# The front of the recurrence and its receptance projection in one stage

## The chip, the cores and the metric

The kernel runs on 1 core of one Trainium2 chip. The metric is the device time of one execution in microseconds; a median over a few executions is compared.

## The reference, cut to what matters

The program computes a first transformer block, then a second model of two layers on 256 latent and 256 context tokens (D = 1024). Each layer ends in a mixture of 32 experts. The second layer's mixer is a bidirectional recurrence; what the change touches is the beginning of `rwkv_prepare`:

```python
h = rmsnorm(x, norm1_g) * (1 + sc1) + sh1          # for latents and for context
xx = h_shift - h                                   # neighbour in the grid, or in the sequence
xr, xw, xk, xv, xa = [h + xx * mu[j] for j in range(5)]
r = xr @ wr                                        # 1024 x 1024, the receptance
k = xk @ wk
v = xv @ wv
lw = tanh(xw @ w1) @ w2                            # per direction; la likewise from xa
```

All is in float32.

## The kernel before, in words

Activations lie with the channels on the partitions: `h`, `xx` and the mixed inputs are `[128, 8, 512]`, eight chunks of 128 channels by 512 tokens. Work is written as a sequence of blocks (stages); each engine runs its own list in a block, and a block ends in a barrier of all engines. `Kernel.clear` (line 216) frees the semaphores of the past stages and adds a second barrier (line 219).

Weights come through a ring of six slots of 1 MB (`Stream`, lines 66 to 128), all loaded from SP's queue in one fixed order of tiles. `feed` starts tile n + 6 when tile n has been used; `hold` stops the stream before a given tile and `resume` (line 101) starts the six held tiles at once. The order here is `rw_wr_2` (four tiles of 256 output columns, slots 0 to 3), `w1` (one tile, two DMAs), `rw_wk_2` (four), `rw_wv_2` (four), `a1`, `g1`, `g2`, `wo`.

The stages around the change, in order of time:

- `experts_stage` for layer 0 (line 2375). It ends in the combination: SP fetches the experts' rows (line 2416), ACT and DVE weigh and add them (2572, 2441), PE turns them (2544), DVE adds them to `k.x` (2454). Its last entry on SP is the resume of the weight stream, which starts `rw_wr_2`'s four tiles, `w1` and the first of `rw_wk_2`. Then comes `k.clear()` (line 2729).
- `rwkv_front` (line 2755). ACT squares the eight chunks (2767), PE sums them into bank 0 with a matrix of ones (2783), DVE and ACT form the inverse root (2818 to 2823), DVE scales each chunk (2827), ACT adds the shift (2776), POOL takes the differences `xx` (2803 to 2812), and DVE blends chunk by chunk into `xm0`, the input of the receptance (2834). SP has nothing to do here.
- `linear_stage` "rw_wr_2" (line 579 on). PE forms the eight output chunks of `r` one after the other, each over all eight input chunks in one bank, four banks in turn (line 623). DVE first computes the next mixed input into `xm1` (`mix`, line 2842, passed as `first`), then copies each finished bank to `r` (2848). SP refills a weight slot each time two output chunks are done.
- `linear_stage` "w1", then "rw_wk_2", "rw_wv_2", "a1", "g1", "g2", and the scan.

One float32 product of 128x128 by 128x512 is recorded as two matmul instructions, so the receptance's 64 products are 128 instructions.

Of the kernel before, what the change touches and what calls it, by code (L numbers as in the profile page):

```python
# [19 lines left out]
ALU = mybir.AluOpType  # L20
# [4 lines left out]
P = 128  # L25
D = 1024
DC = D // P
# [2347 lines left out]
def experts_stage(k, route):  # L2375


    nc, l, TT = k.nc, route.l, route.TT
    ring = k.ring
    pair_rows = k.pair_rows[l]  # L2380
    with ExitStack() as ctx:
# [17 lines left out]
        weighed, summed, cturned, added = (k.sem(f"cb_{n}") for n in ("weighed", "summed", "turned", "added"))  # L2399
        block = ctx.enter_context(nc.Block())  # L2400
        half_cols = lambda bank, t: bank[t * RH:(t + 1) * RH, 0:256]

        @block.sync
        def _(sp):
            for n in range(ring.SLOTS, NE * ring.PIECES):
                e, j = divmod(n, ring.PIECES)
                if n == (AFTER + 3) * ring.PIECES:
                    sp.wait_ge(spent, 4 * AFTER + 4)
                    over.sync(sp)
                done, part = divmod(n - ring.SLOTS, ring.PIECES)  # L2410
                sp.wait_ge(spent, 4 * done + (1, 1, 2, 2, 3, 4)[part])
                ring.start(sp, k.a, l, e, j)
            for s in range(2):
                sp.wait_ge(put[s], 16 * (NE // 2))
            for t in range(TT):
                sp.dma_start(pairs[t], pair_rows[4 * P * t:4 * P * (t + 1), :].rearrange("(p c n) d -> p c (n d)", c=2, n=2))\
                    .then_inc(fetched[t], 16)
            if l == 0:
                k.stream.resume(sp, k.seg["wo"].first)

        @block.vector
        def _(dve):
# [329 lines left out]
    return ["rw_wr_2", "w1", "rw_wk_2", "rw_wv_2", "a1", "g1", "g2", "wo"]  # L2752


def rwkv_front(k, parts, h, xx, sq, scratch, mixed):


    nc = k.nc
    r0, mean, rr = (scratch[:, n, :] for n in range(3))
    squared, summed, meaned, rooted, vdone, scaled, ready, edged = (k.sem(f"front_{n}") for n in (  # L2760
        "squared", "summed", "meaned", "rooted", "vdone", "scaled", "ready", "edged"))
    W, q = 64, DC // 4
    with nc.Block() as block:
        @block.scalar
        def _(act):
            for c in range(DC):
                nc.scalar.activation(sq[:, c, :], k.x[:, c, :], ACT.Square).then_inc(squared, 1)
            nc.scalar.preload_act_table_set("natural_log_exp_and_others")
            act.wait_ge(meaned, 1)
            nc.scalar.activation(r0, mean, ACT.Ln).then_inc(rooted, 1)  # L2770
            act.wait_ge(rooted, 1)
            nc.scalar.activation(r0, r0, ACT.Exp, scale=-0.5).then_inc(rooted, 1)
            for c in range(DC):
                for n, (t0, t1, _, shift) in enumerate(parts):
                    act.wait_ge(scaled, 2 * c + n + 1)
                    nc.scalar.activation(h[:, c, t0:t1], h[:, c, t0:t1], ACT.Identity, bias=shift[:, c:c + 1])\
                        .then_inc(ready, 1)

        @block.tensor
        def _(pe):  # L2780
            for c in range(DC):
                pe.wait_ge(squared, c + 1)
                last = nc.tensor.matmul(k.bank[0][:, :], k.ones[:, :], sq[:, c, :], start=(c == 0), stop=(c == DC - 1))
            last.then_inc(summed, 1)

        @block.gpsimd
        def _(pool):
            for c in range(DC):
                a, b = h[:, c, 0:SEQ], xx[:, c, 0:SEQ]
                rows = lambda x: x.rearrange("p (r w) -> p r w", w=W)  # L2790
                pool.wait_ge(ready, 2 * c + 1)
                if c < q:
                    edge, inner = (rows(b)[:, :, 0:1], rows(a)[:, :, 0:1]), (
                        rows(b)[:, :, 1:W], rows(a)[:, :, 0:W - 1], rows(a)[:, :, 1:W])
                elif c < 2 * q:
                    edge, inner = (rows(b)[:, :, W - 1:W], rows(a)[:, :, W - 1:W]), (
                        rows(b)[:, :, 0:W - 1], rows(a)[:, :, 1:W], rows(a)[:, :, 0:W - 1])
                elif c < 3 * q:
                    edge, inner = (b[:, 0:W], a[:, 0:W]), (b[:, W:SEQ], a[:, 0:SEQ - W], a[:, W:SEQ])
                else:  # L2800
                    edge, inner = (b[:, SEQ - W:SEQ], a[:, SEQ - W:SEQ]), (
                        b[:, 0:SEQ - W], a[:, W:SEQ], a[:, 0:SEQ - W])
                nc.gpsimd.tensor_scalar(edge[0], edge[1], -1.0, None, ALU.mult).then_inc(edged, 1)
                nc.gpsimd.tensor_tensor(inner[0], inner[1], inner[2], ALU.subtract).then_inc(edged, 1)
                a, b, n = h[:, c, SEQ:TB], xx[:, c, SEQ:TB], TB - SEQ
                pool.wait_ge(ready, 2 * c + 2)
                e = 0 if c < DC // 2 else n - 1
                nc.gpsimd.tensor_scalar(b[:, e:e + 1], a[:, e:e + 1], -1.0, None, ALU.mult).then_inc(edged, 1)
                if c < DC // 2:
                    nc.gpsimd.tensor_tensor(b[:, 1:n], a[:, 0:n - 1], a[:, 1:n], ALU.subtract).then_inc(edged, 1)  # L2810
                else:
                    nc.gpsimd.tensor_tensor(b[:, 0:n - 1], a[:, 1:n], a[:, 0:n - 1], ALU.subtract).then_inc(edged, 1)

        @block.vector
        def _(dve):
            link = Chain(dve, vdone)
            dve.wait_ge(summed, 1)
            nc.vector.tensor_scalar(mean, k.bank[0][:, :], 1.0 / D, EPS, ALU.mult, ALU.add).then_inc(meaned, 1)
            dve.wait_ge(meaned, 1)
            dve.wait_ge(rooted, 2)  # L2820
            link(nc.vector.tensor_tensor(rr, r0, r0, ALU.mult))
            link(nc.vector.scalar_tensor_tensor(out=rr, in0=rr, scalar=-0.5, in1=mean, op0=ALU.mult, op1=ALU.mult))
            link(nc.vector.scalar_tensor_tensor(out=rr, in0=rr, scalar=1.5, in1=r0, op0=ALU.add, op1=ALU.mult))
            for c in range(DC + 2):
                if c < DC:
                    for t0, t1, gain, _ in parts:
                        nc.vector.scalar_tensor_tensor(out=h[:, c, t0:t1], in0=k.x[:, c, t0:t1],
                                                       scalar=gain[:, c:c + 1], in1=rr[:, t0:t1],
                                                       op0=ALU.mult, op1=ALU.mult).then_inc(scaled, 1)
                if c >= 2:  # L2830
                    b = c - 2
                    dve.wait_ge(ready, 2 * b + 2)
                    dve.wait_ge(edged, 4 * b + 4)
                    nc.vector.scalar_tensor_tensor(out=mixed[:, b, :], in0=xx[:, b, :], scalar=param(k, "mu", 1, b),
                                                   in1=h[:, b, :], op0=ALU.mult, op1=ALU.add)


def mix(k, xx, h, n, to, T=TB):

    def run(dve):  # L2840
        for c in range(DC):
            k.nc.vector.scalar_tensor_tensor(out=to[:, c, 0:T], in0=xx[:, c, 0:T], scalar=param(k, "mu", 1, n * DC + c),
                                             in1=h[:, c, 0:T], op0=ALU.mult, op1=ALU.add)
    return run
# [6 lines left out]
def rwkv(k, held, more):  # L2851
    nc, a, seg = k.nc, k.a, k.seg
    with ExitStack() as outer:
# [6 lines left out]
        with ExitStack() as c2:  # L2860
# [1 line left out]
            xm1 = c2.enter_context(nc.sbuf_tensor("rw_mixed1", [P, DC, TB], F32))  # L2862
            h, xx, xm0 = (c3.enter_context(nc.sbuf_tensor(f"rw_{n}", [P, DC, TB], F32)) for n in ("h", "xx", "mixed0"))
            parts = [(t0, t1, k.gain1[:, n, :], k.mod[:, n, 0:DC]) for n, (t0, t1) in enumerate([(0, SEQ), (SEQ, TB)])]
            rwkv_front(k, parts, h, xx, xm0, xm1, xm0)

            for n, name, dst in ((0, "rw_wr_2", r), (1, "w1", lw), (2, "rw_wk_2", kx), (3, "rw_wv_2", v),
                                 (4, "a1", la)):
                xm = (xm0, xm1)[n % 2]
                following = mix(k, xx, h, n + 1, (xm0, xm1)[(n + 1) % 2], TB if n < 4 else SEQ)  # L2870
                if name in ("w1", "a1"):
                    f = ACT.Tanh if name == "w1" else ACT.Copy
                    linear_stage(k, name, seg[name], whole_tiles(DC, P), lambda f, xm=xm: xm[:, f, :], TB,
                                 lambda act, m, ps, f=f, dst=dst: nc.scalar.activation(dst[:, :], ps[:, :], f), 4,
                                 on_scalar=True, first=following)
                else:
                    linear_stage(k, name, seg[name], whole_tiles(DC, 256), lambda f, xm=xm: xm[:, f, :], TB,
                                 copy_to(nc, dst), 4, first=following)
# [933 lines left out]
```

## Time and profile before

| | |
|---|---|
| median of 3 runs | 3166.9 us (3159.68 to 3167.87) |
| the profiled execution | 3166.59 us, of which the span of the trace is 3164.9 us |
| TensorE (PE) busy | 2720.3 us, 86% of the span |
| VectorE (DVE) busy | 1071.8 us, 34% |
| ScalarE (ACT) busy | 528.0 us, 17% |
| GpSimd (POOL) busy | 325.0 us, 10% |
| DMA | 638.61 MB, mean 202 GB/s |
| mean granted TensorE clock | 0.948 of 2.4 GHz |

Busy shares are averages over some forty stages with different limits. What matters for a change in two of them is a view in order of time: which engine ends last in each, and what the next stage's first instruction waits for. "Idle before, releaser" in brackets gives how long an engine stood still before an instruction and what ended that; a q behind an engine's name (PEq, DVEq) is its sequencer, so "PEq L219" stands for a barrier at line 219.

### The profile page before, as it was taken

What the parts mean: (1) busy time and instruction counts of PE and PEld (TensorE: products, weight loads), DVE (VectorE), ACT (ScalarE), POOL (GpSimd) and SP (SyncE); (2) the same over time, 40 slices, a digit from 0 to 9 for tenths busy, and PEclk for the clock granted to TensorE, in tenths of its full rate; (3) what the DMA queues carried; (4) which work ended last, traced back from release to release, by engine and by line L of the source; (5) the groups of instructions that cost most, each with busy time, mean ns of one, the idle gap of its engine ahead of it and who ended that gap; (6) DMA issues with size and microseconds to landing.
All of it is one profiled execution on the core that took longest, in us unless ns stands there. A gap on an engine that the chain in (4) does not pass through costs nothing. (4 is left out here: it accounts for less than half of the span.)

```text
span 3164.9 us, 59020 instructions
## 1 busy us (share of the span) xinstructions
PE 2720.3 (86%) x25835; PEld 1973.8 (62%) x25835; DVE 1071.8 (34%) x2214; ACT 528.0 (17%) x1149; POOL 325.0 (10%) x358
## 2 busy tenths in 40 slices
PE   8999999989999997878776599798899987977775
PEld 7886766678868775444443244588788874544443
DVE  4563337435733213101001421465556422100002
ACT  1001132300011002000000100344444312000001
POOL 1000000000000001111110200223222202111110
PEclk9999999989999997989999799799999988999997
DMA  7785432057865237999998220000000138999994
GB/s 259 241 245 159 121 123 94 29 184 248 264 202 150 70 102 296 395 401 402 401 406 330 91 80 23 20 4 4 3 4 4 57 131 319 405 407 408 406 406 180
DMA packets 297238, 638.61 MB, mean 202 GB/s; under 512 B 29252, under 2 KB 198423, under 8 KB 262436
## 3 DMA queue, kind: packets, MB, share of 16 engines
q1 hardware_dynamic: 254896, 558.44, 48.3%
q10 hardware_dynamic: 30500, 61.96, 5.4%
q0 software_dynamic: 11600, 14.59, 1.5%
q8 instruction: 199, 3.26, 0.4%
q14 instruction: 43, 0.35, 0.0%
HBM read 634.79 MB, written 21.08 MB: 207 GB/s over the span
## 5 line engine op out<-in xcount | busy, mean ns | idle before, releaser
L2509 PE MATMUL bank<-expert_weights,ex_xt 128*64 128x256 f32 x2560 | 306.0, 386 | 79.9 <-DMA expert_weights<-in_moe_w_up_dram 61.5
L544 PE MATMUL bank<-u,weights 128*128 128x272 f32 (+1 forms) x1408 | 319.2, 390 | 12.0 <-DVEq L567 12.0
L2509 PEld LDWEIGHTS bank<-expert_weights,ex_xt 128*64 128x64 f32 x2560 | 203.2, 139 | 186.5 <-issue 121.0
L544 PEld LDWEIGHTS bank<-u,weights 128*128 128x128 f32 x1408 | 271.1, 193 | 59.9 <-DVEq L567 12.6
L1353 DVE SCALAR_TENSOR_TENSOR ada_acc<-ada_w,cond,ada_acc 128x512 f32 (+1 forms) x336 | 227.7, 747 | 1.6 <-PEq L516 1.6
L2427 DVE TENSOR_TENSOR ex_hidden<-ex_silu,bank 128x256 f32<-128x256 f32 x64 | 27.0, 421 | 572.2 <-ACT ex_silu L2558 572.2
L623 PE MATMUL bank<-rw_mixed,weights 128*128 128x512 f32 (+2 forms) x448 | 188.7, 582 | 31.9 <-DVEq L636 28.2
L2509 PE MATMUL bank<-weights,ex_xt 128*64 128x256 f32 x1280 | 163.1, 394 | 34.1 <-DMA weights<-in_moe_w_up_dram 24.1
L2530 PE MATMUL bank<-expert_weights,ex_hidden_turned 128*64 128x512 f32 x640 | 152.6, 619 | 20.7 <-DVE ex_hidden_turned L2430 20.1
L2558 ACT ACTIVATE ex_silu<-bank 128x256 f32<-128x256 f32 x64 | 24.6, 384 | 872.6 <-PE bank L2509 857.5
L623 PEld LDWEIGHTS bank<-rw_mixed,weights 128*128 128x128 f32 (+1 forms) x448 | 83.9, 189 | 137.1 <-issue 135.2
L623 PE MATMUL bank<-hidden,weights 128*128 128x272 f32 (+1 forms) x704 | 157.2, 386 | 3.8 <-DVEq L636 3.8
L2509 PEld LDWEIGHTS bank<-weights,ex_xt 128*64 128x64 f32 x1280 | 102.7, 142 | 89.4 <-issue 55.3
L623 PEld LDWEIGHTS bank<-hidden,weights 128*128 128x128 f32 x704 | 133.6, 190 | 27.4 <-DVEq L636 4.7
L3748 POOL TENSOR_TENSOR sc_n<-sc_nt,sc_masks 128x512 f32<-128x512 f32 x80 | 103.5, 1295 | 404.2 <-PE bank L3032 257.5
L2434 DVE COPY ex_y<-bank 128x512 f32<-128x512 f32 x64 | 44.3, 692 | 249.5 <-PE bank L2530 249.5
L2370 POOL DMA_INDIRECT rt_xg<-token_rows,rt_tokens x64 | 61.1, 955 | 517.7 <-PE bank L2493 398.7
L2530 PEld LDWEIGHTS bank<-expert_weights,ex_hidden_turned 128*64 128x64 f32 x640 | 43.8, 141 | 103.9 <-issue 74.0
L2462 POOL DMA_INDIRECT pair_rows<-ex_y,rt_pairs_of x64 | 65.6, 1025 | 376.4 <-DVE ex_y L2434 344.9
L3032 PE MATMUL bank<-sc_x,sc_n 64*64 64x64 f32 x2560 | 96.1, 220 | 3.1 <-POOL sc_x L3750 1.9
L3032 PEld LDWEIGHTS bank<-sc_x,sc_n 64*64 64x64 f32 x2560 | 88.7, 136 | 14.1 <-issue 14.1
L2530 PE MATMUL bank<-weights,ex_hidden_turned 128*64 128x512 f32 x352 | 83.7, 617 | 12.9 <-DVE ex_hidden_turned L2430 10.9
(612 smaller groups left out, 4312.7 us busy)
## 6 DMA issues: line engine op xcount, KB each, us to landing
expert_weights<-in_moe_w_gate_dram SPq DMA_DIRECT2D x80, 1024.0 KB
expert_weights<-in_moe_w_up_dram SPq DMA_DIRECT2D x80, 1024.0 KB
expert_weights<-in_moe_w_down_dram SPq DMA_DIRECT2D x80, 1024.0 KB
ada_w<-in_ada_w_dram ACTq DMA_DIRECT2D x24, 2048.0 KB, 9.1
weights<-in_moe_w_down_dram SPq DMA_DIRECT2D x44, 1024.0 KB
weights<-in_moe_w_gate_dram SPq DMA_DIRECT2D x40, 1024.0 KB
weights<-in_moe_w_up_dram SPq DMA_DIRECT2D x40, 1024.0 KB
weights<-in_ga_w_in_dram SPq DMA_DIRECT2D x32, 1024.0 KB, 5.8
```

The lines of the kernel that those rows point to most:

```text
L544: last = nc.tensor.matmul(k.bank[b + side * NB][:, 0:N], w[:, f, c * P:(c + 1) * P], rhs[:, f, 0:N], start=(f == 5), stop=(f == 4))
L623: last = nc.tensor.matmul(ps[:, t0:t1], view(slot), of(r), start=(starts and p == 0), stop=(ends and p == len(pieces) - 1))
L1353: last = nc.vector.scalar_tensor_tensor(out=to, in0=src, scalar=c, in1=to, op0=ALU.mult, op1=ALU.add)
L2370: pool.indirect_dma_start(route.xg[:, e % 2, :], None, route.rows, bass.IndirectOffsetOnAxis(ap=route.tokens[0:SLOTS, e:e + 1], axis=0), b ...
L2427: nc.vector.tensor_tensor(hid[:, s, :], act_out[:, s, :], k.bank[3][:, 0:256], ALU.mult)\
L2434: nc.vector.tensor_copy(y[:, s, :], k.bank[6 + s][:, :]).then_inc(kept, 1)
L2462: pool.indirect_dma_start(pair_rows, bass.IndirectOffsetOnAxis(ap=route.pairs_of[:, e:e + 1], axis=0), y[:, e % 2, :], None, bounds_check= ...
L2509: last = nc.tensor.matmul(half_cols(k.bank[2 + side], t), xt[:, s, f * SLOTS:(f + 1) * SLOTS], w[:, q * 512 + t * 256:q * 512 + t * 256 + ...
L2530: last = nc.tensor.matmul(k.bank[6 + s][n * RH:(n + 1) * RH, :], ht[:, s, o:o + SLOTS], w[:, q * D + n * 512:q * D + n * 512 + 512], start ...
L2558: nc.scalar.activation(act_out[:, s, :], k.bank[2][:, 0:256], ACT.Silu).then_inc(silued, 1)
L3032: last = nc.tensor.matmul(ps[rows, CHUNK(j)], lhsT(rows, j), rhs(rows, j), start=True, stop=True)
L3748: level_mask = lambda z, level: nc.gpsimd.tensor_tensor(chunked(q.n[:, z, :]), chunked(q.nt[:, z, :]), mask_of(q, M_LEVEL + level - 1), AL ...
```

## The change

The front and the receptance projection become one block. The resume of the weight stream moves from the end of the experts' block to SP's list in the new block, followed by the feed of `rw_wr_2`. PE takes the products in another order: for each blended chunk f it adds that chunk's part to all eight output chunks, in banks 0 to 7, and signals the outputs only in the last pass. DVE then computes the next mixed input and copies the eight banks.

```diff
@@ experts_stage, SP, after the pairs' fetches
-            if l == 0:
-                k.stream.resume(sp, k.seg["wo"].first)
@@ rwkv_front
-def rwkv_front(k, parts, h, xx, sq, scratch, mixed):
+def rwkv_front(k, parts, h, xx, sq, scratch, mixed, r, following):
...
+        @block.sync
+        def _(sp):
+            k.stream.resume(sp, k.seg["wo"].first)
+            k.stream.feed(sp, seg, made, lambda j: 2 * j + 2, 2 * seg.tiles)
...
             last.then_inc(summed, 1)
+            for f in range(DC):
+                pe.wait_ge(blended, f + 1)
+                for m in range(DC):
+                    if f == 0 and m % 2 == 0:
+                        k.stream.wait(pe, seg, 0, m // 2)
+                    w = f * 256 + m % 2 * P
+                    last = nc.tensor.matmul(k.bank[m][:, :], k.stream.slot(seg, m // 2)[:, w:w + P], mixed[:, f, :],
+                                            start=(f == 0), stop=(f == DC - 1))
+                    if f == DC - 1:
+                        last.then_inc(made, 1)
...
-                                                   in1=h[:, b, :], op0=ALU.mult, op1=ALU.add)
+                                                   in1=h[:, b, :], op0=ALU.mult, op1=ALU.add).then_inc(blended, 1)
+            following(dve)
+            for m in range(DC):
+                dve.wait_ge(made, m + 1)
+                nc.vector.tensor_copy(r[:, m, :], k.bank[m][:, :])
@@ rwkv
-            rwkv_front(k, parts, h, xx, xm0, xm1, xm0)
-
-            for n, name, dst in ((0, "rw_wr_2", r), (1, "w1", lw), (2, "rw_wk_2", kx), (3, "rw_wv_2", v),
+            rwkv_front(k, parts, h, xx, xm0, xm1, xm0, r, mix(k, xx, h, 1, xm1))
+
+            for n, name, dst in ((1, "w1", lw), (2, "rw_wk_2", kx), (3, "rw_wv_2", v),
```

## Rows read from the trace of the kernel before

**Rows 1.** Busy time by stretch: PE, PEld, DVE, ACT, POOL (us), clock, DMA share, GB/s
```profile
1750.50:1755.20 4.70, 0.00 (x0) 0.00 (x0) 0.00 (x0) 0.00 (x0) 0.00 (x0) 0.50 1.17 312
...
1764.90:1773.40 8.50, 0.01 (x1) 0.00 (x0) 6.34 (x12) 3.87 (x8) 3.03 (x6) 0.80 0.00 0
1773.40:1789.60 16.20, 0.00 (x0) 0.00 (x0) 10.92 (x17) 4.64 (x10) 15.36 (x27) 0.50 0.00 1
```

**Rows 2.** Order of time (start, us, engine, line), from the combination to the front's sum
```profile
1746.26 4.22 DVE L2454 SCALAR_TENSOR_TENSOR x<-bank,mod,x 128x128 f32<-128x128 f32 x16
...
1751.34 2.77 SPq L93 DMA_DIRECT2D weights<-in_rw_wk_dram  x1
1755.21 4.27 ACT L2767 ACTIVATE rw_mixed<-x 128x512 f32<-128x512 f32 x8 [11.69 <-PEq L219]
...
1755.89 9.01 PE L2783 MATMUL bank<-rw_mixed,ones 128*128 128x512 f32 x16 [7.53 <-ACT rw_mixed L2767]
```

**Rows 3.** Order of time, the blends: first, second and eighth of eight
```profile
1772.64 0.75 DVE L2834 SCALAR_TENSOR_TENSOR rw_mixed<-rw_xx,params,rw_h 128x512 f32<-128x512 f32 x1 [0.58 <-ACT rw_h L2776]
...
1775.47 0.84 DVE L2834 SCALAR_TENSOR_TENSOR rw_mixed<-rw_xx,params,rw_h 128x512 f32<-128x512 f32 x1 [0.94 <-POOL rw_xx L2803]
...
1788.87 0.75 DVE L2834 SCALAR_TENSOR_TENSOR rw_mixed<-rw_xx,params,rw_h 128x512 f32<-128x512 f32 x1 [1.31 <-POOL rw_xx L2812]
```

**Rows 4.** Order of time, the receptance's products, last copy, next stage's products
```profile
1790.34 56.91 PE L623 MATMUL bank<-rw_mixed,weights 128*128 128x512 f32 x128 [25.43 <-DVEq L636]
...
1847.29 0.69 DVE L2848 COPY rw_r<-bank 128x512 f32<-128x512 f32 x1 [6.18 <-PE bank L623]
...
1848.44 7.11 PE L623 MATMUL bank<-rw_mixed,weights 128*128 128x512 f32 x16 [1.20 <-ACTq L636]
```

**Rows 5.** The experts' block's end (line 2381), 1749 to 1755.5: ns, then start us
```profile
L2381 DVEq DRAIN x1: 2108/2108/2108, 1748.4 to 1748.4; - x1
L2381 SPq DRAIN x1: 123/123/123, 1754.2 to 1754.2; - x1
```

**Rows 6.** Order of time around the clear before the scan
```profile
2004.25 0.42 DVE L2891 COPY rw_gate<-bank 128x256 f32<-128x256 f32 x1 [1.88 <-PE bank L623]
2005.54 2.08 PE L3150 MATMUL bank<-rw_lw,sc_w 64*128 64x512 f32 x4 [1.33 <-PEq L219]
```

**Rows 7.** Order of time, a DVE result and the PE that waited for it
```profile
1736.05 1.28 DVE L2441 SCALAR_TENSOR_TENSOR expert_weights<-expert_weights,rt_wts 128x1024 f32<-128x1024 f32 x1 [9.47 <-ACT expert_weights L2572]
...
1737.39 1.97 PE L2544 MATMUL bank<-ident,expert_weights 128*128 128x128 f32 x8 [11.55 <-DVE expert_weights L2441]
```

**Rows 8.** Order of time, weight loads early in the receptance's products
```profile
1793.03 0.34 PEld L623 LDWEIGHTS bank<-rw_mixed,weights 128*128 128x128 f32 x1 [0.52 <-issue]
1793.87 0.19 PEld L623 LDWEIGHTS bank<-rw_mixed,weights 128*128 128x128 f32 x1 [0.50 <-issue]
1794.30 0.19 PEld L623 LDWEIGHTS bank<-rw_mixed,weights 128*128 128x128 f32 x1 [0.24 <-issue]
```

**Rows 9.** Busy time by stretch of 2 us, after the front's sum
```profile
1768.00:1770.00 2.00, 0.00 (x0) 0.00 (x0) 1.93 (x4) 0.23 (x1) 0.00 (x0) 0.99 0.00 0
1770.00:1772.00 2.00, 0.00 (x0) 0.00 (x0) 2.00 (x5) 1.77 (x5) 1.63 (x4) 0.50 0.00 0
```

**Rows 10.** SP's four issues for `wo`; DMA share in 0.75 us slices from 2470
```profile
2477.09 5.43 SPq L93 DMA_DIRECT2D weights<-in_rw_wo_dram  x4
...
DMA  0000000000179999999999999994100000000000
```

**Rows 11.** DMA issues, 1800 to 1850: count, KB, us from issue to landing
```profile
weights<-in_rw_wk_dram SPq DMA_DIRECT2D x3, 1024.0 KB, 5.2
```

**Rows 12.** Order of time, one expert: products over two banks, products in one
```profile
1711.48 3.67 PE L2509 MATMUL bank<-expert_weights,ex_xt 128*64 128x256 f32 x32 [1.44 <-DMA expert_weights<-in_moe_w_up_dram]
...
1722.18 3.65 PE L2530 MATMUL bank<-weights,ex_hidden_turned 128*64 128x512 f32 x16 [0.52 <-DVE ex_hidden_turned L2430]
```

**Rows 13.** Groups of instructions, 1789.6 to 1847.9: busy us, mean ns of one
```profile
L623 PE MATMUL bank<-rw_mixed,weights 128*128 128x512 f32 x128 | 56.9, 607 | 25.4 <-DVEq L636 25.4
```

More of the change, by code:

```diff
@@ L2752, in rwkv_segments @@
     return ["rw_wr_2", "w1", "rw_wk_2", "rw_wv_2", "a1", "g1", "g2", "wo"]
-def rwkv_front(k, parts, h, xx, sq, scratch, mixed):
-    nc = k.nc
+def rwkv_front(k, parts, h, xx, sq, scratch, mixed, r, following):
+    nc, seg = k.nc, k.seg["rw_wr_2"]
     r0, mean, rr = (scratch[:, n, :] for n in range(3))
-    squared, summed, meaned, rooted, vdone, scaled, ready, edged = (k.sem(f"front_{n}") for n in (
-        "squared", "summed", "meaned", "rooted", "vdone", "scaled", "ready", "edged"))
+    squared, summed, meaned, rooted, vdone, scaled, ready, edged, blended, made = (k.sem(f"front_{n}") for n in (
+        "squared", "summed", "meaned", "rooted", "vdone", "scaled", "ready", "edged", "blended", "made"))
     W, q = 64, DC // 4
     with nc.Block() as block:
+        @block.sync
+        def _(sp):
+            k.stream.resume(sp, k.seg["wo"].first)
+            k.stream.feed(sp, seg, made, lambda j: 2 * j + 2, 2 * seg.tiles)
         @block.scalar
```

## The prediction

> **What bounds the kernel now.** The page says that PE is busy for 86% of the span, but not where the rest is lost, so I read the stretches around the changed lines first [rows 1]. From 1750.5 to 1755.2 no engine computes and only the DMA engines move data. From 1764.9 to 1789.6 DVE, ACT and POOL work and PE stands still. From 1790.3 on PE is busy for 56.9 us without a gap [rows 4]. Each stretch has one owner, and they stand one behind another: first a barrier, then the vector side of the front, then PE.
>
> Next I read the order of time for what ends each stretch. The combination's last sum of `k.x` ends at 1746.26 + 4.22 = 1750.48, yet the front's first square starts only at 1755.21, released by the barrier of line 219; in between SP is still issuing the sixth held tile, until 1751.34 + 2.77 = 1754.11 [rows 2]. The block's own end says who is late: DVE's drain, which begins at 1748.4 and lasts 2.108 us, is over at 1750.5, and SP's begins at 1754.2 [rows 5]. So it is SP's issuing, not computing, that ends the experts' block.
>
> In the front the first blend is done at 1772.64 + 0.75 = 1773.39 and the eighth at 1789.62 [rows 3]. The receptance needs all eight only because of its order of work. Its 128 instructions run from 1790.34 to 1847.25, the last copy ends at 1847.98, and the next stage's PE starts at 1848.44 [rows 4].
>
> **Part 1, the resume leaves the experts' block.** Without SP's seven issues that block ends with DVE at 1750.48. From the last work to the first instruction behind a clear it took 1755.21 - 1754.11 = 1.10 us here [rows 2], and 2005.54 - 2004.67 = 0.87 us at the clear before the scan, where DVE was last as it will be here [rows 6]. I take 0.9: the front's first square starts at 1751.4, which is 3.8 us earlier (3.6 to 3.9 by the two rows). The fetches of the experts' rows stand ahead of the resume on the same queue, so I cost their landing at no change. From below the price of Part 1 is nothing, if POOL or ACT turned out to be as late as SP; no row shows that.
>
> The issues themselves are not gone: SP makes them at the head of the new block, where it has nothing else to do until PE's last pass. Nobody waits for SP there, only for the landings. The nearest row is `wo`: four 1 MB tiles issued into an empty queue. It took SP 5.43 us from 2477.09, and the DMA engines were busy until the slice that ends at 2491.75, 14.7 us after the first issue [rows 10]. By that the fourth receptance tile is there at 1751.4 + 14.7 = 1766.1. The first product is due at 1769.7 (below) and the seventh, the first that needs the fourth tile, later still. So the cost is nothing, with 3.5 us in hand. If the loading ran at half that pace, 29.4 us, the fourth tile would come at 1780.8; the first pass, slow as it starts, wants it 4 x 0.84 + 8 x 0.43 = 6.8 us after 1769.7, at 1776.5. That is a loss of some 4 us, and my upper bound for this part.
>
> During 1751 to 1771 the loads now lie beside squares, sum, and the first scales and differences. Before, they lay beside the combination and the squares, and eight squares took 4.27 us all the same [rows 2]. I cost this at nothing, within 0.5 us either way.
>
> **Part 2, products follow the blended chunks.** Everything in the front from the first square to the first blend keeps its order: 1773.39 - 1755.21 = 18.18 us. So blend 0 is done at 1751.4 + 18.2 = 1769.6. PE follows a DVE result within 1737.39 - 1737.33 = 0.06 us [rows 7], so products start at 1769.65 in place of 1790.34: 20.7 us earlier, of which 3.8 are Part 1's and 16.9 this part's.
>
> Does PE then run through? One warm instruction takes 1794.30 - 1793.87 = 0.43 us, a cold one 1793.87 - 1793.03 = 0.84 [rows 8]. A pass of 16 takes 6.9 us warm. The second blend is done 2.9 us behind the first and the eighth 16.2 behind it, 2.3 us each on the mean [rows 3], so PE is the slower from its first pass: blend 1 is ready 2.9 us after the start, pass 1 begins 4 x 0.84 + 12 x 0.43 = 8.5 us after it. The eight waits on `blended` find their value already there, as do the waits on the four tiles. The same number of waits (each output chunk's bank and each tile) stood in the old order, whose 128 instructions show no gap. Thus the products take 56.9 us as before: the same 128 instructions and as many weight loads, the same slow start.
>
> The slow start stays because PE still rests before it. The granted clock was 0.99 of full speed until 1770 and 0.50 from then on, 5 us after the sum's last product [rows 9]. The new gap is from 1761.1 to 1769.65, 8.5 us, so the first instructions again run at 1.2 GHz, and four of them cost 4 x 0.41 = 1.7 us extra, already inside the 56.9. Were PE still warm, the time would be 1.7 us lower; this is the lower bound of the term.
>
> Eight banks in place of four, and a new bank with each product: the nearest rows are an expert's. Its gate and up products alternate between two banks and take 3.67 / 32 = 0.115 us per 256 columns; its down products stay in one bank and take 3.65 / 16 = 0.228 per 512, the same per column [rows 12]. I cost switching at nothing. At the other end, the switch could lose the overlap between neighbours; that end is priced as a rival.
>
> The Trainium skill has two rules that speak against this loop. "TensorE: Matmul & The Clock Gate", section "HAM oscillation", advises finishing all K-tiles of an output before waiting, since a wait between K-tiles lets the clock fall in every one; its section on psum-queue depth-cycling says the same of cycling through banks with small pauses. Here the row shows the chunks coming faster than PE uses them, so the first has nothing to bite on; by either, the time would be that of the clock rival below.
>
> **Part 3, the tail of the stage.** DVE's next mix (8 instructions) starts right after blend 7, at about 1786, and ends by 1792, far before the first finished bank. Copies of 0.69 us follow outputs that now finish every 0.86 us (two instructions), so only the last copy is behind PE, as before: the stage ends 0.73 us after its last product [rows 4]. The barrier between front and receptance (0.3 us and the first wait) is gone, and is inside the 20.7.
>
> The cost of the new order is in the refills. All four slots come free in the last 5.2 us, at 1.7 us steps, where they came free 13.7 us apart. So four tiles of 1 MB are issued together; SP's last issue falls at the end of the products. [rows 10] say what four such issues take: 5.43 us from the first. These start 5.2 us before the end, so SP is free some 0.3 us after PE, before DVE's last copy; the barrier doesn't move. They are all landed 14.7 us after the first, 9.5 us into what follows. The stage `w1` uses a tile landed long ago and takes 7.1 us [rows 4]. The stage behind needs its first tile, which is the sixth held one, and its second only after another pass of 13.7 us. A single tile landed 5.2 us after its issue [rows 11]. So no wait there: cost nothing, at most 1 us if SP's last issue is held longer than in [rows 10].
>
> **Sum.** 3.8 + 16.9 = 20.7 us less. The profiled execution took 3166.6 us (span 3164.9 and 1.7 around it), so it becomes 3145.9. It lies 0.3 us under the median of the runs shown, so the forecast for a median is 3146.
>
> **Rivals.**
>
> *The barrier does not move (chance 0.07).* Some other engine or the clear itself holds the front until 1755.2. For it: idle barriers are put down to PE's sequencer in the view, which names no true culprit. Against it: SP's drain in [rows 5]. Only Part 2 is left: 3166.6 - 16.9 = 3149.7 us.
>
> *Weights late, or slower vector work beside the loads (0.06).* The bound above, 4 us: 3145.9 + 4 = 3149.9 us.
>
> *Switching banks costs (0.03).* An instruction is recorded with 0.607 us on the mean [rows 13], though they start 0.43 apart, since neighbours overlap. If nothing overlapped, 128 x (0.607 - 0.43) = 22.7 us would be added: 3145.9 + 22.7 = 3168.6 us, no gain. Against it, [rows 12].
>
> *The clock stays down, the case on the other side (0.03).* If the passes were broken by waits, so that PE stayed at 1.2 GHz, each of the 124 warm instructions would take 0.41 us more, 51 us in all: 3145.9 + 51 = 3197 us. From 50 slow instructions more on (20.7 / 0.41) the change loses. For it: in the front PE does fall to half speed when it rests. Against it: blends every 2.3 us on the mean against passes of 6.9 us. The Trainium skill's two sections named above would have this one come.
>
> **How the numbers follow.** The forecast has 0.81, the four rivals 0.07, 0.06, 0.03 and 0.03. A measurement of this kernel can't tell less than about 0.3% from no change, 9.5 us (the three runs shown lie 8.2 us apart). Forecast and the first two rivals are faster by more: 0.94. The banks' case is no change, 0.03, and the clock's slower, 0.03. For the range: above, the first two rivals reach 3150, and I add 1 us for SP's last issue; below, a warm start gives 3144, and the lowest run of before lay 7 us below the median, which puts a like one at 3139. Range 3139 to 3151.
>
> **What would show it.** ACT's first square about 0.9 us behind the last sum of the combination; SP's seven issues behind it; a product of the new line starting 18.2 us after that square, with 128 instructions in 57 us and no idle time between; clock 0.5 for its first 3.5 us and then 1.0; four refills in its last 5.2 us; `w1` starting 1.2 us after it. The prediction is wrong if the square stays at 4.7 us behind the sum, if products wait for weights, if PE idles or runs cold between passes, or if the key projection waits for its second tile.

## The result and the profile after

| | before | after |
|---|---|---|
| the pair timed first (4 runs each) | 3166.56 us (3159.68 to 3167.87) | 3134.03 us (3130.67 to 3139.49) |
| ratio | | 0.9904, 95% interval 0.989 to 0.9918 |
| the same two, second time (17 and 6 runs) | 3165.34 us | 3144.81 us, ratio 0.9936 (0.9916 to 0.9956) |
| third time (11 and 6 runs) | 3166.8 us | 3140.08 us, ratio 0.9924 (0.9906 to 0.9942) |
| profiled execution | 3166.59 us, span 3164.9 | 3139.49 us, span 3137.8 |

The change is faster, by 32.5 us in the first comparison. Over all five comparisons (two of them stand only among the experiments) the median of the changed kernel's 16 executions is 3139.5 us, and that of the 78 of the kernel before is 3165.7: 26 us, where 21 were forecast. Single executions of one kernel lie up to 20 us apart. Much of that arises ahead of the change: in the 16 profiles kept, the first fetch of the combination, with the same code ahead of it in all, starts anywhere from 1722.7 to 1740.5 us. The range of 3139 to 3151 misses the first median by 5 us.

In order of time, the new stage shows first how its block begins (start, us, engine, line); this answers to [rows 2].

```profile
1745.37 4.22 DVE L2452 SCALAR_TENSOR_TENSOR x<-bank,mod,x 128x128 f32<-128x128 f32 x16
...
1750.54 6.37 SPq L93 DMA_DIRECT2D weights<-in_rw_wr_dram  x4
1750.56 4.27 ACT L2770 ACTIVATE rw_mixed<-x 128x512 f32<-128x512 f32 x8 [7.97 <-PEq L219]
1751.24 9.64 PE L2786 MATMUL bank<-rw_mixed,ones 128*128 128x512 f32 x16 [3.77 <-ACT rw_mixed L2770]
```

The last sum ends at 1749.59 and the first square begins 0.97 us later; it was 4.73. SP's issues now stand beside ACT. Next the first blend, the products and the end of the stage, answering to [rows 3] and [rows 4]:

```profile
1768.61 0.75 DVE L2847 SCALAR_TENSOR_TENSOR rw_mixed<-rw_xx,params,rw_h 128x512 f32<-128x512 f32 x1 [0.57 <-ACT rw_h L2779]
...
1769.41 57.16 PE L2794 MATMUL bank<-rw_mixed,weights 128*128 128x512 f32 x128 [8.53 <-DVE rw_mixed L2847]
...
1826.60 1.47 SPq L93 DMA_DIRECT2D weights<-in_rw_wv_dram  x1
...
1828.67 7.11 PE L623 MATMUL bank<-rw_mixed,weights 128*128 128x512 f32 x16 [2.11 <-SPq L2761]
```

PE starts 0.05 us behind the first blend, waits nowhere, and takes 57.16 us for its 128 instructions. The next stage's PE comes 2.10 us behind the last product where it came 1.19 us behind before, and its releaser is SP. The drains of that barrier (line 2761; us of the start at the end of each line) say the same:

```profile
L2761 DVEq DRAIN x1: 706/706/706, 1826.6 to 1826.6; - x1
L2761 SPq DRAIN x1: 139/139/139, 1828.1 to 1828.1; - x1
```

The busy time by stretch (PE, PEld, DVE, ACT, POOL, clock, DMA share, GB/s), answering to [rows 1], shows DVE and ACT beside the moved loads and PE beside the blends:

```profile
1760.90:1769.40 8.50, 0.00 (x0) 0.00 (x0) 6.37 (x12) 3.87 (x8) 3.06 (x6) 0.63 1.07 297
1769.40:1826.60 57.20, 57.16 (x128) 25.03 (x128) 21.04 (x32) 4.64 (x10) 15.32 (x27) 0.97 0.08 26
```

From the first fetch of the combination to the first product of `w1` it is 118.4 us before (1730.04 to 1848.44) and 99.6 after (1729.04 to 1828.67). That is 18.8 of the 27.1 us between the two profiled executions. 1.0 us is a drift ahead of the stage. Nearly all of the rest, 7.2 us, lies 140 us behind it, in g2, whose code the change doesn't touch. Its products in the two traces, before and then after:

```profile
1986.98 17.23 PE L623 MATMUL bank<-rw_gate_hidden,weights 128*128 128x256 f32 x32 [1.42 <-DVEq L636]
```

```profile
1967.00 10.07 PE L623 MATMUL bank<-rw_gate_hidden,weights 128*128 128x256 f32 x32 [1.42 <-DVEq L636]
```

The same 32 instructions behind the same rest of 1.42 us differ by 7.2 us. The clock column tells why. The kernel before, around its g2:

```profile
1986.00:1988.00 2.00, 1.02 (x4) 0.59 (x4) 0.50 (x2) 0.00 (x0) 0.00 (x0) 1.00 0.00 0
1988.00:1990.00 2.00, 2.00 (x6) 0.84 (x4) 0.42 (x1) 0.00 (x0) 0.00 (x0) 0.60 0.00 0
1990.00:1992.00 2.00, 2.00 (x4) 1.00 (x4) 0.42 (x1) 0.00 (x0) 0.00 (x0) 0.50 0.00 0
```

And the changed kernel:

```profile
1966.00:1968.00 2.00, 1.00 (x4) 0.59 (x4) 0.50 (x2) 0.00 (x0) 0.00 (x0) 1.00 0.00 0
1968.00:1970.00 2.00, 2.00 (x8) 0.89 (x6) 0.84 (x2) 0.00 (x0) 0.00 (x0) 1.00 0.00 0
```

Before, the granted clock falls to 1.2 GHz 1.4 us after g2's first product and stays there for all of it; after, g2 runs at 2.4 GHz, and the same fall comes 11.2 us after its first product, when g2 is over. Below, "slow" and "fast" g2 stand for these two. Behind g2 nothing more is won or lost: the first products of the scan start at 2005.54 before and 1978.40 after, 27.1 us apart, and PE's last group starts at 3156.75 and 3129.64, again 27.1.

### The profile page after: what moved, and what is told of

The parts are those of the page before. It is cut to its first block and busy times, and to the rows that moved or that the text cites. A ratio compares the mean times of both kernels' runs of the same rounds, so it can differ in the third digit from the quotient of the medians.

```text
span 3137.8 us, 59005 instructions
## 1 busy us (share of the span) xinstructions
PE 2718.9 (87%) x25835; PEld 1972.3 (63%) x25835; DVE 1071.0 (34%) x2214; ACT 527.7 (17%) x1149; POOL 324.4 (10%) x358
## 5 line engine op out<-in xcount | busy, mean ns | idle before, releaser
L623 PE MATMUL bank<-rw_mixed,weights 128*128 128x512 f32 (+2 forms) x320 | 131.8, 572 | 7.2 <-DVEq L636 2.8
L623 PEld LDWEIGHTS bank<-rw_mixed,weights 128*128 128x128 f32 (+1 forms) x320 | 59.0, 186 | 80.3 <-issue 78.5
L3049 PE MATMUL bank<-weights 64*64 64x64 f32 x2304 | 89.7, 223 | 4.8 <-DVE weights L3510 3.6
```

The source lines that it names most:

```text
L623: last = nc.tensor.matmul(ps[:, t0:t1], view(slot), of(r), start=(starts and p == 0), stop=(ends and p == len(pieces) - 1))
L3049: last = nc.tensor.matmul(ps[rows, CHUNK(j)], lhsT(rows, j), rhs(rows, j), start=True, stop=True)
```

## The experiments

All times are medians in us; the kernel before was timed beside each, and its median stands with the ratio. An idle product is one whose result nobody uses; it only keeps PE busy.

**The two parts by themselves, and g2's clock.** `e1` has only the moved resume:

```diff
 experts_stage:  -            if l == 0:
                 -                k.stream.resume(sp, k.seg["wo"].first)
 rwkv_front:     +        @block.sync
                 +        def _(sp):
                 +            k.stream.resume(sp, k.seg["wo"].first)
```

> Only the resume of the weight stream is moved into the front's block; the receptance keeps its own stage and its order. Theory A (the change's two parts are worth 3.8 and 16.9 us as forecast, and the rest of the gain, some 7 us, is the stage g2 whose products ran at half clock in the profile of before, 17.2 us, and at full clock in that of after, 10.1 us, according to when it comes): the first square follows the last sum of the combination by 0.9 us in place of 4.7, the receptance takes 57 us as before, and the time is 3163 us with a slow g2 or 3156 with a fast one, nothing between. Theory B (the moved loads themselves are worth more than forecast, up to 15 us, because they lay across the combination): combination shorter than 20.4 us from the first fetch to the last sum, time near 3150 whatever g2 does.

`e2` is the changed kernel with the resume back in the experts' block:

```diff
 experts_stage:  +            if l == 0:
                 +                k.stream.resume(sp, k.seg["wo"].first)
 rwkv_front:     -            k.stream.resume(sp, k.seg["wo"].first)
```

> One stage with products following the chunks, but the resume stays at the end of the experts' block. Theory A: 16.9 us from products that start behind the first blend, minus 0.9 for the last refill's issue that ends the stage late; the square comes 4.7 us behind the last sum; the time is 3150.5 us with a slow g2, 3143.5 with a fast one. Theory B (all of the surplus over the forecast belongs to the new order): 3139 us or less with g2 slow as before.

`e3` and `e4` are the kernel before and the changed one with idle products in the rest between g1 and g2:

```diff
+        def idle_products(n):
+            for _ in range(n):
+                nc.tensor.matmul(k.bank[7][:, 0:SEQ], k.ones[:, :], k.x[:, 0, 0:SEQ], start=True, stop=True)
+            idle_products(keep[0])        # head of PE's list; keep=(1, 0) in g2
...
+            idle_products(keep[1])        # end of it; keep=(0, 1) in g1
```

> The kernel before, with one idle product (128x128 by 128x256, result unused, into bank 7) at the end of g1 and one at the head of g2, where PE rests 1.4 us between the two stages. Theory A: PE's clock stays up, g2's products take 10.1 us in place of 17.2, the time is 3159.5 us, and the spread between executions of this kernel narrows to a few us. Rival C (g2's slowness comes from its products, half of which have only 32 rows, or from weights, not from the rest before them): g2 stays at 17.2 us or falls back within it, time 3166 us.

> The changed kernel with the same two idle products. Theory A: g2 was already at full clock in its profile, so the time stays within 2 us of the changed kernel's 3134 us, 20 us under the kernel before with the same fill. Rival C: same time too. Theory B or another cause of the surplus: the distance to the filled kernel before stays 30 us or more.

| | median, runs | before | ratio (95%) | g2's products in the profile |
|---|---|---|---|---|
| e1 | 3160.5, 12 | 3166.9 | 0.9979 (0.9968 to 0.999) | 17.0 us |
| e2 | 3145.0, 6 | 3166.9 | 0.9934 (0.9915 to 0.9953) | 10.1 |
| e3 | 3159.3, 12 | 3166.9 | 0.9976 (0.9964 to 0.9988) | 10.1 |
| e4 | 3137.4, 6 | 3166.9 | 0.9912 (0.9895 to 0.9929) | 10.1 |

In e1's profile the first square comes 0.98 us behind the last sum (0.97 in the changed kernel), and from first fetch to last sum it is 20.5 us against 20.4 before: theory B's shorter combination isn't there. From the first fetch to `w1`'s first product e1 is 3.1 us shorter than before and e2 16.0; the sum, 19.1, is close to the 18.8 of both together, so the parts add up. e1's time was forecast to be 3163 with a slow g2 or 3156 with a fast one and nothing between; it is 3160.5, between the two, so time alone can't show g2's state at this spread. e2 lies 1.5 us above the 3143.5 of a fast g2, which its profile shows; theory B wanted 3139 or less with a slow one. The idle products gave the kernel before 7.6 us (3159.3, forecast 3159.5), though its executions still spread over 14 us where a few were forecast. They left the changed kernel, over all its executions (below), where it was, while this first median was 3.4 us above the first of the changed kernel. With them in both, the two differ by 21.8 us, where theory B wanted 30 or more and the forecast for the stage was 20.7. The surplus over the forecast is g2's clock.

**Chance, code or place.** The changed kernel was timed again, and delays were put in the front's chain, ahead of the products:

```diff
 rwkv_front, DVE, behind rr:
+            for _ in range(2):            # 4 in e6, on the changed kernel
+                link(nc.vector.tensor_tensor(scratch[:, 3, :], mean, mean, ALU.mult))
```

> The changed kernel once more, for its spread beside the others. Theory A (stage worth some 20 us, g2 at full clock worth 7 us more): 3134 to 3138 us, like the changed kernel with idle products (3137.4). If g2's clock is a matter of chance in each execution, a second cluster 7 us above it; the median then 3138 to 3141.

> The kernel before with two more DVE operations of 0.7 us each in the front's chain, 1.4 us of pure delay on the path. Theory A1 (the clock is reviewed at moments tied to the program's start, so that shifting g2 decides whether its rest of 1.4 us is taken for idleness): g2 moves out of the slow place, and the longer kernel is faster, 3161 us, g2 10.1 us in the profile. Theory A2 (the moments are not tied to the program, g2's state is drawn anew in each execution or set by what stands before it): 3166.9 + 1.4 = 3168 us.

> The changed kernel with four such operations, 2.9 us of delay, which puts g2 where it stood against the clock's changes in the profile of before. Theory A1: g2 is slow again, 3134 + 2.9 + 7.2 = 3144 us or a little more. Theory A2: 3137 to 3140 us, and g2 fast or slow as it falls.

The changed kernel gave 3144.8 us this time (6 runs from 3131.2 to 3149.8), more than any expectation had; e5 3167.2 against 3165.3, ratio 1.0008 (0.9996 to 1.002), g2 slow in the profile; e6 3143.2 (5 runs), ratio 0.9933 (0.992 to 0.9947), g2 fast. Theory A1, as I had put it, fell: g2 kept its state in both, and the clock's changes stood elsewhere against the program's start in each trace. (e6's time alone is what A1 had forecast, 3144; its profile is what speaks against it.)

`e8` asks the clock 24 times in one execution. Behind g2 a stage repeats the products of a1, g1 and g2 with rests between them; its core:

```diff
+            for n in range(REPEATS):      # 24
+                ...                       # 8 products 128x128 by 128x512, rest()
+                ...                       # 8 of 128x128, 8 of 128x32, by 128x256, rest()
+                for m in range(8):
+                    for c in range(2):
+                        rows = (P, 32)[c]
+                        last = nc.tensor.matmul(k.bank[4 + m % 4][:, 0:SEQ], q.w2[0:rows, m * P:(m + 1) * P],
+                                                k.x[0:rows, m, 0:SEQ], start=(c == 0), stop=(c == 1))
+                rest(last)
```

> The changed kernel with a stage added behind g2 whose results are unused: 24 times over the products of a1 (8 of 128x128 by 128x512), a rest, those of g1 (8 of 128x128 and 8 of 128x32 by 128x256), a rest of about 1.4 us, and those of g2 (8 of 128x128 and 8 of 32x128 by 128x256). The first rest is about 1.3 us in the odd repetitions and shorter in the even ones. It asks whether the code decides g2's clock or the moment does. Theory A2 (the moment: the same products behind the same rest are taken at full clock or fall to half, by where they lie against the clock's reviews): of 24 identical repetitions some take 10 us and some 15 to 17, within one trace, in both lengths of the first rest. Theory D (the code: the first rest, 1.29 us in traces with a slow g2 and 1.09 in those with a fast one, decides): all repetitions with the longer rest slow, all with the shorter fast.

Two of the 24, neighbours, PE in order of time:

```profile
2552.84 16.38 PE L2899 MATMUL bank<-x,sc_w 128*128 128x256 f32 x32 [1.50 <-DVEq L2911]
...
2590.00 10.10 PE L2899 MATMUL bank<-x,sc_w 128*128 128x256 f32 x32 [1.50 <-DVEq L2911]
```

23 repetitions took 16.1 to 17.5 us and one 10.1, with the same code and the same rest. Eleven of the twelve with the shorter first rest were slow like the twelve with the longer. So the code alone doesn't decide (theory D fell), and the moment does, as A2 had it. In the 23 the clock fell 1.2 to 2.8 us behind the first product. The moment is not without order, though: the repetition of 10.1 us began 14.2 us behind the clock's last rise, the shortest distance of all; 22 of the others began 14.3 to 15.9 us behind it, and one 42.1.

The same trace holds the kernel's own g2, and that is neither fast nor slow:

```profile
1967.43 12.03 PE L623 MATMUL bank<-rw_gate_hidden,weights 128*128 128x256 f32 x32 [1.42 <-DVEq L636]
```

Here the clock fell 7.7 us behind the first product, and only the last 4.4 us of g2 ran at 1.2 GHz.

> The changed kernel again, since its two medians so far are 3134.0 and 3144.8 us and lie 11 us apart, each on a chip and a day of its own beside the kernel before (3166.6 and 3165.3). With the stage worth 20 us and g2's clock drawn in each execution: between 3136 and 3146 us, single executions spread over 15 us.

> The changed kernel with idle products around g2's start, on the same chip as the run of the changed kernel. If its g2 is slow in some executions, the fill takes these away: 2 to 4 us under the changed kernel. If never, equal within 2 us.

The changed kernel: 3140.1 us; with idle products 3141.3, both with ratio 0.9924. The 12 executions with them have the median 3139.2, the 16 without 3139.5: nothing to gain there. They are no safe cure either: in this profile g2 took 15.2 us in spite of them.

**Where it comes from.** The distance in time from the clock's last rise to g2's first product sorts the profiles, with one between (theory E). Each rise is taken from stretches of 0.25 us; that of the changed kernel lies in the second of these two:

```profile
1771.00:1773.00 2.00, 2.00 (x4) 0.69 (x3) 1.56 (x3) 0.33 (x2) 2.00 (x4) 0.50 0.02 4
1773.00:1775.00 2.00, 2.00 (x6) 0.99 (x5) 2.00 (x4) 0.86 (x3) 2.00 (x5) 0.91 0.00 0
```

| profile, no idle products | last rise | g2's first product | distance | g2 |
|---|---|---|---|---|
| e1 | 1801.41 | 1994.32 | 192.9 | slow |
| before | 1793.85 | 1986.98 | 193.1 | slow |
| e9 (below) | 1765.98 | 1959.13 | 193.2 | slow |
| e5 | 1796.21 | 1989.53 | 193.3 | slow |
| after | 1773.38 | 1967.00 | 193.6 | fast |
| e8, its own g2 | 1773.70 | 1967.43 | 193.7 | 12.0 us |
| e6 | 1785.78 | 1979.61 | 193.8 | fast |
| after, third | 1764.97 | 1959.12 | 194.2 | fast |
| after, second | 1771.53 | 1965.86 | 194.3 | fast |
| e10 (below) | 1794.93 | 1989.36 | 194.4 | fast |
| e2 | 1777.66 | 1972.45 | 194.8 | fast |

In the four profiles with a slow g2 the clock fell 1.2 to 1.7 us behind g2's first product, in the six with a fast g2 10.4 to 13.4 us behind it, when g2 was over: it falls in all of them, and what differs is whether g2 is still running. The rise lies in the receptance's products, early on. From there PE runs at full clock through stages of fixed length (`w1`'s to g2's first product: 138.3 to 138.5 us in all eleven), so the distance hardly depends on anything ahead, e5's and e6's delays included. The new order lengthens it by what SP's last issue adds to the end of the stage. The rows other than e9's and e10's were there when this was formed, but I had overlooked e8's own g2, so the "without exception" in e9's expectation was too strong. Three kernels tested it. `e9` makes the last refill in the next stage:

```diff
-            k.stream.feed(sp, seg, made, lambda j: 2 * j + 2, 2 * seg.tiles)
+            for t in range(seg.tiles - 1):
+                sp.wait_ge(made, 2 * t + 2)
+                k.stream.start_number(sp, seg.first + t + RING)
...                                       # and start_number(..., 3 + RING) as `early` of stage "w1"
```

`e10` and `e11` lengthen the kernel before behind the rise:

```diff
 stage "rw_wr_2", DVE, behind the last copy:
+            def late(dve):
+                link = Chain(dve, k.sem("late"))
+                for n, w in enumerate((512, 256)):        # (512, 512, 512, 256) in e11
+                    link(nc.vector.tensor_tensor(v[:, n, 0:w], h[:, n, 0:w], h[:, n, 0:w], ALU.mult))
```

> The changed kernel with one edit: the fourth refill, whose issue by SP held the end of the new stage for about 1 us, is made at the head of the next stage. Theory E (the clock's fall in g2 is set by how long g2 begins after the clock's last rise, which lies in the receptance's products: 192.9 to 193.3 us in the four profiles with the old order of stages, slow in the three of them without idle products; 193.6 to 194.8 us in those of the changed kernel and its variants, fast without exception where no idle products were added): with the 1.1 us gone the distance is 193.0 us again, g2 takes 17 us, and the kernel is slower for an edit that takes time away: 3139.5 - 1.1 + 7.2 = 3145.6 us. Theory A2 (g2's state is a matter of chance in each execution): 3138.5 us.

> The kernel before with two chained DVE operations (128x512 and 128x256), about 1.2 us, at the end of the receptance's stage, behind the clock's last rise. Theory E: the distance becomes 194.3 us, g2 is fast, and the kernel with more work is faster: 3166.2 + 1.2 - 7.2 = 3160 us. Theory A2: 3167.4 us.

> The same with four operations, about 2.6 us. Theory E: the distance is 195.7 us; in the trace with 24 repetitions g2's products were slow wherever the clock changed 1.2 to 2.8 us behind their start, and this distance puts them back there, so g2 is slow again: 3166.2 + 2.6 = 3168.8 us. A theory that a longer pause as such helps: 3162 us or less. Theory A2: 3168.8 as well.

e9's profile, products' end, next stage and g2 in order of time:

```profile
1762.88 56.72 PE L2796 MATMUL bank<-rw_mixed,weights 128*128 128x512 f32 x128 [8.54 <-DVE rw_mixed L2849]
1820.80 7.11 PE L623 MATMUL bank<-rw_mixed,weights 128*128 128x512 f32 x16 [1.19 <-ACTq L636]
...
1959.13 17.24 PE L623 MATMUL bank<-rw_gate_hidden,weights 128*128 128x256 f32 x32 [1.43 <-DVEq L636]
```

And e10's:

```profile
1850.83 7.11 PE L623 MATMUL bank<-rw_mixed,weights 128*128 128x512 f32 x16 [2.48 <-ACTq L636]
...
1989.36 10.07 PE L623 MATMUL bank<-rw_gate_hidden,weights 128*128 128x256 f32 x32 [1.43 <-DVEq L636]
```

In both, g2 is where the place says: taking 0.9 us away from the changed kernel made g2 slow, adding 1.3 to the kernel before made it fast. They also rule out theory D's first rest in the kernel itself, ahead of g1: it is 1.09 us in e9, whose g2 is slow, and 1.29 in e10, whose g2 is fast. e9 took 3143.2 us (6 runs) against 3163.3, ratio 0.9938 (0.9924 to 0.9953), 20 us off as forecast from a slow g2; the interval also touches the changed kernel's 0.9924, so time alone would not tell. e10 took 3160.5 (12 runs) against 3163.3, ratio 0.9997 (0.9983 to 1.0011), between -6 and +1.2 and in favour of neither. e11 missed: 3164.3 (12 runs), ratio 1.0006 (0.9996 to 1.0016), and g2 was fast. Behind its pause of 3.94 us the clock fell 0.7 us after `w1`'s first product, `w1` took 8.8 us in place of 7.1, and the last rise came only at 1851.64, so the distance was another one, 136.2 us. Its forecast, that g2 is slow again at 195.7 us, was thus not tested.

**Together.** `e7` has e4's idle products, e9's refill and nine idle products between the front's sum and the first product:

```diff
             last.then_inc(summed, 1)
+            for n in range(9):
+                nc.tensor.matmul(k.bank[7][:, :], k.ones[:, :], k.x[:, n % DC, :], start=True, stop=True)
```

> The changed kernel with three additions: the two idle products around g2's start; nine idle products (128x128 by 128x512) between the front's sum and the first product, where PE rests 8.5 us; and the last of the four refills issued in the next stage's block instead of this one's. Theory A: products start at full clock, 55.0 us in place of 57.2; the next stage's PE starts 1.2 us behind the last product in place of 2.1; g2 stays at 10.1. Together 3 us under the changed kernel with idle products alone, 3134.5 us. A rival: the idle products delay the first product, since nine of them take 7.7 us at full clock but more at half, and PE is late by up to 4 us: 3138 us or more.

3137.0 us (6 runs; forecast 3134.5, its rival 3138 or more), ratio 0.9921 (0.9903 to 0.9939). Its profile has what was meant. The nine idle products take 7.9 us behind the sum, and the first product still comes 0.06 us behind the first blend:

```profile
1769.04 55.20 PE L2805 MATMUL bank<-rw_mixed,weights 128*128 128x512 f32 x128 [0.82 <-DVE rw_mixed L2858]
```

The products take 55.2 us in place of 57.2, and `w1` follows 1.19 us behind them. But 3 us are less than these comparisons resolve; the changed kernel's own ratios run from 0.9904 to 0.9936.

## Why the prediction was right or wrong

*What bounds it, and Part 1: right.* SP's issuing held the experts' block. The barrier part gave 4.73 - 0.97 = 3.76 us (forecast 3.8).

*Loads at the head of the new block: right.* No product waited for weights, and from the sum's end to the first blend's start it took 7.7 us in both traces, with the DMA engines full beside it.

*Part 2: right, 0.9 us short.* Square to first product is 18.85 us (forecast 18.25), because the sum took 9.64 us in place of 9.01: the clock rose later in it. The products took 57.16 (56.9). No pass waited and the clock held at 0.97, so the Trainium skill's rule against waiting between K-tiles ("TensorE: Matmul & The Clock Gate", "HAM oscillation") didn't bite: its case has an idle PE between tiles, this one has none.

*Part 3: the term I set at nothing, at most 1 us, was 0.9 us.* I had taken the 5.43 us of [rows 10] from the first issue on, as if four issues took as long in all when each waits for its slot. But the fourth can only be made when the last product is done, and then it counts in full: it took 1.47 us, where the three before it took 0.37 each. In e9 the same issue, made 1.3 us after the last product, took 0.37 us, so what lengthens it is the loads issued just before.

*The stage's sum: right in the main.* The profiled pair gave 18.8 us of the 20.7; the 0.6 of the sum, 0.3 of the products and 0.9 of the last issue are the difference. From the first fetch to g2's first product it is 257 to 258 us in profiles of the old order (before, e3) and 236.4 to 239.0 in six of the new one: 20.0 us on the mean.

*The step that failed is the last sentence of the sum, "so it becomes 3145.9".* It took everything behind the stage as unchanged. One term was missing, worth up to 7.2 us: g2's products in the profile of before ran at half clock, which the clock column of that trace showed and I read for the front alone. The 0.9 us of Part 3 moved g2 out of the place where the clock falls: with them taken away (e9) g2 took 17.2 us again. So the mistake in Part 3 and the missing term are one chain. With g2 alike in both kernels (e3 and e4) the difference is 21.8 us.

*The rest of the miss is sampling.* The first four runs of the changed kernel were low: 3134.0 against 3139.5 over all 16. That pooled median lies at the low end of my range. I had taken the spread of three runs for that of the kernel. Nor is it a merit that the pooled median is inside: the range reached that low for a warm start and for a lucky draw, and not for a faster g2.

*The rivals.* Barrier unmoved, weights late, bank switching and a clock held down by the passes were all refuted by the first profile. None of them was about the clock behind the stage.

**Open.** Why g2's products, half of them with 32 rows, let the clock fall where others don't is not shown. The length of the rest alone isn't it: the clock fell at 1.4 us of rest ahead of g2 and stayed up at 2.1 to 2.7 us ahead of `w1` (after, e10, e2). Nor does PE's rest alone make the fall: it fell in g2 once with idle products in the rest. That the distance decides rests on ten profiles, two of them forecast, with an eleventh between; why e8's fall came in the middle of g2 at 193.7 us, and the changed kernel's behind it at 193.6, is open. The timed executions agree with it in the mean but give no state of their own. Those of the kernel before need not all be slow; in the last comparison nine of 23 lay at 3157 to 3160 us.

## What to carry to other kernels

Before adding up a saving, list the stretches behind the change in which PE is busy at half clock: a shift of 1 us can move them in or out, and here it was worth a quarter of the change. When a change's gain exceeds its sum, compare stage by stage also where the code is the same; then test with a shift, not with a story. When slots are released together at the end of a stage, the last issue holds the barrier (0.9 us here). It can be given to the next stage, but in e9 that moved g2 back to half clock, and the kernel was no faster for it.

## What the runs showed of the hardware

- The same 32 products behind the same rest of 1.5 us ran at full clock once and at half 23 times in one execution (10.1 against 16.1 to 17.5 us).
- In one profile each, a kernel with 0.9 us less waiting had a slower g2, and one with 1.3 us more a faster one.
- The clock fell 1.2 to 1.7 us behind g2's first product in four profiles, where g2 took 17.0 to 17.4 us, and 10.4 to 13.4 us behind it in six, where g2 took 10.1.
- Rests of 2.1 to 2.7 us ahead of `w1` left the clock up; 3.94 us let it fall 0.7 us after the next product began.
- Four 1 MB loads issued 1.7 us apart held SP 1.47 us in the fourth issue (1.47 to 2.07 in eight profiles); the three before it, and single ones, 0.37 us.
